# A transformer block pair on one core: late projection chunks between the first attention pairs, the product with V between a pair's transposes

## The reference

```
h = rms_norm(x);  qa, ka, va, qb, kb, vb = split(h @ w_in)        # 12 chunks of 128 columns
qa, ka = rope(rms_norm per head);  qb, kb = rope                  # 8 + 8 query heads, 2 + 2 kv heads of 64
out_a = softmax(qa ka' / 8) va                                    # all 512 keys
out_b = softmax over |kpos - qpos| <= 128, with a sink logit per head
mixed = concat(rms_norm(out_a), rms_norm(out_b)) @ w_out          # the two group norms
x = x + rms_norm(mixed);  x = x + rms_norm(ffn(rms_norm(x)))
second block: pooling and stick-breaking attention, gated ffn, x = x + sigmoid(rms_norm(x) @ w) * (p @ w_p)
result = rms_norm(x)
```

## Time and profile before

| | us |
|---|---|
| median of three runs | 1353.02 |
| the profiled execution | 1354.36 |
| its span in the trace | 1350.8 |
| TensorE matmul busy | 1317.9 (98%) |
| VectorE busy | 663.6 (49%) |
| ScalarE busy | 540.3 (40%) |
| GpSimd busy | 114.2 (8%) |

### The profile page before, as it was taken

One profiled execution on the slowest core, in us unless ns is written; L12 is line 12 of the kernel. 1 busy time (PEld: TensorE's weight loads), 2 busy tenths in 40 slices (PEclk: granted clock), 3 DMA queues, 4 the chain that ended last, 5 costly groups with the idle time before them and its releaser, 6 DMA issues.

```text
span 1350.8 us, 14769 instructions
## 1 busy us (share of the span) xinstructions
PE 1317.9 (98%) x6132; PEld 1054.4 (78%) x6132; DVE 663.6 (49%) x905; ACT 540.3 (40%) x733; POOL 114.2 (8%) x112
## 2 busy tenths in 40 slices
PE   6988989999999999999999999999999999999997
PEld 5863458888888888887888888888888888888876
DVE  6768754663535441226535445563544444423246
ACT  6547864542323232225225555542432232322235
POOL 3000113400000001003000001011000000000112
PEclk9999999999999999999999999999999999999999
DMA  6110012032232323231322111222232222232321
GB/s 246 63 63 1 1 60 98 32 125 94 94 97 98 107 65 107 86 127 39 132 94 67 62 64 61 91 96 102 96 108 99 94 94 94 69 102 93 110 94 63
DMA packets 20593, 117.73 MB, mean 87 GB/s; under 512 B 2480, under 2 KB 2864, under 8 KB 9904
## 3 DMA queue, kind: packets, MB, share of 16 engines
q1 hardware_dynamic: 19104, 113.75, 24.6%
q10 hardware_dynamic: 1424, 3.06, 0.6%
HBM read 114.70 MB, written 2.10 MB: 86 GB/s over the span
## 4 chain that ended last, share of the span: by engine, by line
PE 94%; DVE 3%; ACT 1%; DMA 1%; issue 0%; POOL 0%; SPq 0%; ACTq 0%; POOLq 0%
PE ps L477 91%; PE ps L684 2%; DMA w_raw<-weights 1%; DVE prob L1364 1%; DVE nmax L1560 1%; DVE w_lo L1360 1%; POOL sqsum L453 0%; ACT w_hi L921 0%; ACT OUT L921 0%; DVE hf L1367 0%; DVE hf L1360 0%; ACT hf L921 0%; PE ps L560 0%; PE ps L552 0%; ACT sq L921 0%
## 5 line engine op out<-in xcount | busy, mean ns | idle before, releaser
L477 PE MATMUL ps<-h_hi,w_hi 128*128 128x512 f32 (+1 forms) x1256 | 493.3, 393 | 13.1 <-DVE w_lo L1360 12.0
L477 PE MATMUL ps<-h_lo,w_hi 128*128 128x512 f32 (+1 forms) x1256 | 488.6, 389 | 0.0
L477 PE MATMUL ps<-h_hi,w_lo 128*128 128x512 f32 (+1 forms) x1256 | 488.5, 389 | 0.0
L1360 DVE TENSOR_TENSOR w_lo<-w_raw,w_hi 128x2048 fp32r<-128x2048 f32 (+2 forms) x117 | 242.1, 2072 | 274.0 <-ACT w_hi L921 274.0
L477 PEld LDWEIGHTS ps<-h_hi,w_hi 128*128 128x128 f32 x1256 | 236.6, 188 | 66.8 <-issue 13.2
L921 ACT ACTIVATE w_hi<-w_raw 128x2048 fp32r<-128x2048 f32 (+2 forms) x117 | 201.2, 1722 | 199.6 <-DMA w_raw<-weights 199.4
L477 PEld LDWEIGHTS ps<-h_hi,w_lo 128*128 128x128 f32 x1256 | 236.5, 188 | 49.3
L477 PEld LDWEIGHTS ps<-h_lo,w_hi 128*128 128x128 f32 x1256 | 236.6, 188 | 48.7 <-issue 1.0
L453 POOL TENSOR_TENSOR sqsum<-sqsum,sq 128x512 f32<-128x512 f32 x66 | 95.8, 1451 | 987.4 <-ACT sq L921 985.6
L477 PE MATMUL ps<-mid_hi,w_hi 128*128 128x512 f32 x352 | 136.9, 389 | 0.0
L477 PE MATMUL ps<-mid_lo,w_hi 128*128 128x512 f32 x352 | 136.9, 389 | 0.0
(11 more groups left out here) (183 smaller groups left out, 1083.4 us busy)
## 6 DMA issues: line engine op xcount, KB each, us to landing
w_raw<-weights SPq DMA_DIRECT2D x81, 1024.0 KB, 4.9
w_raw<-weights SPq DMA_DIRECT2D x32, 704.0 KB, 4.1
X<-x_t SPq DMA_DIRECT2D x3, 512.0 KB, 8.3
c<-constants ACTq DMA_DIRECT2D x1, 1280.0 KB, 8.8
w_raw<-weights SPq DMA_DIRECT2D x4, 256.0 KB, 8.3
wp_raw<-weights SPq DMA_DIRECT2D x1, 1024.0 KB, 6.9
out<-OUT SPq DMA_DIRECT2D x4, 256.0 KB, 2.7
out<-OUT ACTq DMA_DIRECT2D x4, 256.0 KB, 2.7
```

The costliest lines, as they stand in the source:

```text
L477: return nc.tensor.matmul(out, lhsT, rhs, start=start, stop=stop, skip_group_check=loose)
L1360: return nc.vector.tensor_tensor(out, a, b, op)
```

## The change

The last three projection chunks leave the line and stand between the first pairs: chunk 9 whole in step 0, chunks 10 and 11 in halves of four input tiles in steps 2, 4, 6 and 8, in banks 7, 6, 7. The first two score pairs come right after chunk 8. Rope of chunk 8 also becomes pieces in the loop. The splits of the first two output projection units move: on ScalarE to steps 1 and 4, on VectorE to the end of the loop. From step 11 on, `weighted` runs at odd steps, that is between the two transposes of a pair. The sums of squares of the two group norms no longer go through GpSimd: TensorE adds each tile with eight one-column matmuls (`sum_part`), for group a in steps 45 to 48, for group b two in steps 60 and 62 and two after the loop; the third and fourth square wait for the sums before the previous one. The last product with V waits for the last transposed rows, and not for a copied output. At the end SP issues all eight stores in the order (0,0), (1,0), (0,1), ...; the last half's square moves to VectorE; GpSimd adds one tile less and TensorE one more; VectorE's second half of factors comes before its second output.

```diff
-NORM_A_STEP = 44
+NORM_A_STEP = 43
+SQUARES_B = (60, 62)
+LATE_BANKS = (7, 6, 7)
+LATE_PARTS = {0: (9, 0, 8), 2: (10, 0, 4), 4: (10, 4, 8), 6: (11, 0, 4), 8: (11, 4, 8)}
-LATE_ROPE, LATE_TR, LATE_V = {9: 4, 10: 13}, 23, 25
+LATE_ROPE, LATE_TR, LATE_V = {8: (2, 3, 3, 4), 9: (4, 5, 6, 6), 10: (7, 8, 8, 9)}, 23, 25
...
@@ SP
-            for n, (b, part) in enumerate(((1, 0), (1, 1), (3, 0), (3, 1))):
+            for n, (b, part) in enumerate(((0, 0), (0, 1), (2, 0), (2, 1))):
+                sp.wait_ge(out_act, n + 1)
+                sp.dma_start(*store(b, part)).then_inc(out_stored, 16)
                 sp.wait_ge(out_ready, n + 1)
-                sp.dma_start(*store(b, part)).then_inc(out_stored, 16)
+                sp.dma_start(*store(b + 1, part)).then_inc(out_stored, 16)
@@ TensorE
+            def sum_part(nm, j):
+                pe.wait_ge(*nm.squares(j + 1))
+                for b in range(NB):
+                    last = mm(ps[:, nm.ss_bank, b:b + 1], sq[:, j % 2, b * P:(b + 1) * P], ones[:, 0:1],
+                              j == 0 and b == 0, True, loose=True)
+                last.then_inc((nm.total if j == nm.n - 1 else nm.summed).sem, 1)
...
-            for u in range(1, UNITS_IN1):
-                unit("in1", u, 2 * u, 2, KS, h_hi, h_lo, after=beside, hooks={11: {4: lambda: scores(0)}})
+            for u in range(1, UNITS_IN1 - 1):
+                unit("in1", u, 2 * u, 2 if u < 4 else 1, KS, h_hi, h_lo, after=beside)
+            scores(0)
+            scores(1)
+            def late_part(j, k0, k1):
+                u = j // 2
+                if k0 == 0:
+                    if j == 9:
+                        pe.wait_ge(*n_mix_pre.factor_used)
+                    elif j == 10:
+                        pe.wait_ge(lo_ready, u)
+                        pe.wait_ge(roped, ROPED.index(NORMED[-1]) + 1)
+                    else:
+                        pe.wait_ge(evac_act, EVAC["in1", 9][1])
+                for k in range(k0, k1):
+                    last = three(BANK["in1", j], u % SLOTS, j % 2 * KD + k, h_hi[:, k, :], h_lo[:, k, :],
+                                 k == 0, k == KD - 1)
+                if k1 == KD:
+                    last.then_inc(group_done, 1)
...
-                if s >= 10 and s % 2 == 0:
-                    weighted((s - 10) // 8, (s - 10) % 8 // 2)
+                if s in LATE_PARTS:
+                    late_part(*LATE_PARTS[s])
+                if s == 0:
+                    spread_heads(len(NORMED) - 1)
+                if s >= 10 and s % 2:
+                    weighted((s - 11) // 8, (s - 11) % 8 // 2)
...
-                if s == NORM_A_STEP + 4:
-                    total(n_group_a)
+                if 2 <= s - NORM_A_STEP < 6:
+                    sum_part(n_group_a, s - NORM_A_STEP - 2)
+                if s in SQUARES_B:
+                    sum_part(n_group_b, SQUARES_B.index(s))
...
-                pe.wait_ge(ot_ready, 8)
-                total(n_group_b)
+                sum_part(n_group_b, 2)
+                sum_part(n_group_b, 3)
...
+            pe.wait_ge(*n_final.squares(KD - 1))
+            final_part(0, sq[:, 0, :])
+            final_part(1, sq[:, 0, :])
@@ ScalarE
             def square(nm, j, src):
                 if j >= 2:
-                    act.wait_ge(*nm.summed(j))
+                    act.wait_ge(*nm.summed(j - 1 if nm.kind == "split" else j))
...
+                if s == 4:
+                    split(UNITS_IN1 + 1)
                 if s == 1:
+                    split(UNITS_IN1)
+                    evacuate(9)
+                if s == 5:
+                    evacuate(10)
+                if s == 9:
                     evacuate(11)
...
+                if s + 2 in SQUARES_B:
+                    square_group(n_group_b, 4, SQUARES_B.index(s + 2))
...
-                act.wait_ge(out_act, b + part + 1)
-                act.dma_start(*store(b, part)).then_inc(out_stored, 16)
-            half_square(1)
@@ VectorE
-            split(UNITS_IN1 + 1)
+                if s == 1:
+                    finish_normed(LATE1 - 2)
...
+            split(UNITS_IN1)
+            split(UNITS_IN1 + 1)
             variance(n_group_b, 4 * P)
...
+            dve.wait_ge(half_added, 2)
+            dve.wait_ge(*n_final.squares(KD))
+            tt(sq[:, 1, half_of(1)], X[:, KD - 1, half_of(1)], X[:, KD - 1, half_of(1)], ALU.mult
+               ).then_inc(n_final.squares.sem, 1)
             half_variance(0)
             half_scale(1)
             half_factors(0)
             half_variance(1)
             dve.wait_ge(*n_final.root(1))
             turned_out(1, 0)
+            half_factors(1)
             turned_out(1, 1)
-            half_factors(1)
```

More of the change, by code:

```diff
@@ L294, in __init__ @@
                  self.hi, self.lo) = (Count(norm_sems[e], norm_counts[e]) for e in NORM_EVENTS)
-                self.sums = n + (kind == "wide")
+                self.kind = kind
+                self.sums = n - 1 if kind == "split" else n - (kind == "final") + (kind == "wide")
                 n_f32 = {"split": n, "late": 1, "wide": 1, "added": n, "final": 0}[kind]
@@ L329, in build @@
                 bank = j + 2 if phase in ("ff1", "in2") and 4 <= j < 6 else j % banks
+                if phase == "in1" and j >= LATE1:
+                    bank = LATE_BANKS[j - LATE1]
                 if phase == "in2" and j >= 14:
@@ L364, in vee_bank, with spread_bank @@
             return 4 if j < LATE1 else SIDE_BANK
+        def spread_bank(n):
+            return 4 if n < len(NORMED) - 1 else HSUM_BANK
         def tr_bank(s):
@@ L445, in sum_squares @@
             def sum_squares(nm):
+                if nm.kind == "split":
+                    return
                 if nm.before is not None:
@@ L858, in _ @@
                      hooks={2: {3: lambda: wide_total(n_ple)}})
+            sqsum_all = sqsum[:, :]
             def final_part(i, src):
@@ L862, in final_part @@
                     last = mm(ps[:, SUM_BANKS[i], b:b + 1], src[:, b * P:(b + 1) * P], ones[:, 0:1],
-                              src is sums and b == 2 * i, True, loose=True)
+                              src is sqsum_all and b == 2 * i, True, loose=True)
                 return last
@@ L886, in _ @@
                         turn(b, 0)
-            sums, square = sqsum[:, :], sq[:, 1, :]
-            pe.wait_ge(*n_final.summed(KD))
-            final_part(0, sums)
-            final_part(1, sums)
+            square = sq[:, 1, :]
+            pe.wait_ge(*n_final.summed(KD - 1))
+            final_part(0, sqsum_all)
+            final_part(1, sqsum_all)
+            pe.wait_ge(*n_final.squares(KD - 1))
+            final_part(0, sq[:, 0, :])
+            final_part(1, sq[:, 0, :])
             pe.wait_ge(*n_final.squares(KD))
@@ L1043, in evacuate @@
                 af(y_of(j), ps[:, BANK["in1", j], :], ACT.Copy).then_inc(evac_act, 1)
-            for j in range(11):
-                if j in (3, 5, 7, 9):
+            for j in range(LATE1):
+                if j in (3, 5, 7):
                     split(j // 2 + 2)
@@ L1544, in _ @@
             late_marks = {}
-            for j in range(1, LATE1):
+            for j in range(1, LATE1 - 1):
                 rope(j)
```

65 lines of the change are left out of this document (35 added, 30 removed).

## The result

The changed kernel took 1357.58 us (median of 5 runs, 1357.49 to 1359.28); the kernel before, beside it, 1352.88 us (5 runs, 1352.28 to 1354.19). The ratio is 1.0036, 95% interval 1.0026 to 1.0047: slower by about 4.7 us, where 1353.7 was forecast. The profiled execution took 1359.28 us (span 1357.2), 1.7 above the median.

A forecast was written before the change was run, and what follows sets the result against it. TensorE was taken to bound the kernel, so only its idle time and its work could matter. Terms -8.7 + 2.2 + 2.7 + 3.2 + 0.5 + 0.8 = +0.7 gave 1353.7 us, range 1349.5 to 1357.5.

The forecast's parts named there:

- Part 1: Three projection chunks moved into the first attention pairs fill TensorE's hole at the front: -8.7 us.
- The second rival: ScalarE late in the early pairs behind a late weight landing for split 7: +2.1, 1355.8 or more; chance 0.18.
- Part 2: Product with V between the transposes: +2.2 us in steps 10 to 31, +2.7 in windowed steps 32 to 63.
- the windowed steps: Steps 32 to 63 outside the group sums: pairs bound by TensorE and pairs after copies lose time, +2.7 us.
- The 0.17 ahead of a product after transposes: In each full pair, a load after transposes starts 0.17 us late; the pair takes 3.28 us instead of 3.10.
- waits behind a copied output: Every eighth step, ScalarE's output copy delays the exponential and stalls TensorE: 0.53 us, and 0.78 at step 25.
- Part 3: Group sums on TensorE: +3.2 us for group a, with ScalarE's squares waiting for sums, and +0.5 for group b.
- the second wait of a square: Group a: ScalarE's fourth square waits for TensorE's sum one step after the third: another 1.0 us.
- Group b: Two of its sums on TensorE at steps 60 and 62, partly offset by shorter waits: +0.5 us.
- Part 4: The end: with DMA engines full, the first store is issued later, from one queue: +0.8 us.
- The alternative put beside it: By issue time alone, the end would come 0.8 us earlier and the whole sum 1.6 lower.
- Third, the clock: Rival: clock falls to half in a stretch like 176.9 to 185.2, adding 5.3 us of TensorE work: 1359; chance 0.04.

The follow-up runs named there:

- the kernel with both edits: Changed kernel with group a's squares 2 and 3 in buffers of their own and four 256-column matmuls in each of steps 46 and 47: 1353.48 us.
- the two fills: Changed kernel plus, in each of steps 46 and 47, four 256-column matmuls (1354.47 us) or nine one-column matmuls (1363.31 us).
- own buffers: Changed kernel with group a's third and fourth square in buffers of their own, so ScalarE does not wait for TensorE's sums: 1353.24 us.
- GpSimd's sum: Changed kernel with group a's four squares summed by GpSimd again and one TensorE reduction after step 48: 1349.19 us.
- the old order, product first: Changed kernel with the product with V ahead of both transposes again, at even steps from 10 on: 1349.18 us.
- only the chunks: Only three projection chunks moved between the first pairs; product ahead of both transposes, both groups summed by GpSimd, end as before: 1346.01 us.

## Why the prediction was wrong

**Part 1** was right: -9.1 for -8.7. TensorE works without a hole from 72 to 100. The second rival, a late landing, did not happen.

**Part 2** was right. Steps 10 to 31 cost +2.0 for +2.2, and the windowed steps 1.7 (32 to 43) and 0.8 (50 to 54 at full clock, 6.34 for 5.51), 2.5 for 2.7. The 0.17 ahead of a product after transposes is nearly all there: 3.24 for the 3.28 worked out. The first two waits behind a copied output were 0.44 and 0.70, for 0.53 and 0.78.

**Part 3** was right where the clock was full. The transposes of step 46 came at 5.38 for 5.4. Group b: 1138.95 for 1138.36, +0.6 for +0.5. The loads, with whatever the new order costs there, come to 1.1 for 1.7 in the kernel with both edits; the second wait of a square has no price at full clock, and I leave the term at 3.2.

**Part 4** was right: +0.75 for +0.8. The alternative put beside it, an end 0.8 earlier by issue time, did not come: seven ends as in the changed kernel are 0.75 later than six as before. The Trainium skill (Trainium Kernel Development and Optimization, Key Constraints) says only that several issuers save issue time, and the traces agree with it: from the first store to the end passed 6.9 us with one queue as with two, in all profiles but one. No run changed the number of queues by itself.

**What failed is the rival "Third, the clock", and with it the sum, which takes every term at clock 1.00.** It had 0.04, placed in the stretch that VectorE owns, with the argument that the old rows show 1.00 through transposes, one-column sums and 3 us of idle time. They did, each by itself. The prediction looked for no other place, though the change put two extra waits, sixteen more one-column loads and small transposes next to each other; there the clock fell for 17 us. Its price: steps 44 to 50 took 17.29 for 12.6, steps 50 to 54 took 7.93 for the 6.34 at full clock: 4.7 + 1.6 = 6.3, and 1.6 more in the profiled execution's end. With the measured terms, -9.1 + 2.0 + 2.5 + 3.2 + 0.6 + 0.75, the change at full clock is worth 0.0; with the clock +6.3. The runs show +4.7. Of the difference, 0.5 to 1 is time around the span (below); the rest is likely the start, which two profiles can't settle. The forecast of 1353.7 is what the terms give at full clock to within 0.7, so the sum failed by the clock alone.

That the clock is the cause and not a by-product is shown by the two fills: more work and full clock, 1354.5; as much more work in one-column matmuls, 1363.3. That the fall needs the wait of the squares is refuted by the kernel with own buffers. GpSimd's sum, own buffers and the old order, each by itself, made the fall shorter or rarer, and none kept its profile at 1.00, so what share the waits, the one-column loads and the order have is not shown. What stays open is why one kernel falls in some executions and not in others (own buffers, product first, only the chunks), and why the kernel before, whose steps 54 to 58 take the same 7.95, was at 1.00 in both of its profiles.

## What to carry to other kernels

A row of tiny matmuls on TensorE can cost more than its own time, and by the runs here a stall likely can too, because the matmuls behind it may run at half clock: price an edit that thins TensorE's work twice, once at each clock, and give the second a real chance even where each ingredient is seen at full clock in the old trace. Work moved onto the critical engine to spare an idle one (here GpSimd's adds) needs its reason measured; here putting it back was worth 8.4 us. Where a wait can't be removed, a few wide matmuls into unused columns in it were free where they fitted, and likely paid for themselves; where they did not fit (four in each of steps 46 and 47) they cost 1.5 and gave back more.

## What the runs showed that was not expected

**Half clock outlasts what went ahead of it.** In the changed kernel TensorE was idle for 0.97 us ahead of the fall and for 0.41 in it, busy 15.59 of 16 us, and the clock came back only at 178. The kernel with one-column fills was busy 20.00 of 20.00 us at 0.50.

**An early fall, and where the start lies.** Eleven of the fourteen profiles, both of the kernel before among them, have one more stretch of 3.4 us at half clock ahead of the pairs, which the rows of the attention stage don't show. In the kernel before it ran from 34.2 to 37.6 with TensorE busy all the time, in its second profile from 21.2 to 24.6. In the five profiles with it at 33 or 34 us P lies at 73.2 to 73.9, in the other nine at 70.7 to 72.1. So most of the 2 us by which the start moves goes with where this fall lies; no run set it on purpose.

**Something outside the span.** Device time less span was 1.7 to 2.1 us in each run of eleven kernels, but 2.0 to 4.7 in those of the kernel before (medians 2.43, 2.88 and 2.74 in the three groups) and 2.5 to 3.5 in those with only the chunks moved. In the windows of the kernel before the DMA engines move something more after the span's end at 1350.8 (last columns: share, GB/s); the changed kernel has the like ahead of its stores:

```profile
1352.00:1353.00 1.00, 0.00 (x0) 0.00 (x0) 0.00 (x0) 0.00 (x0) 0.00 (x0) 0.50 0.00 0
1353.00:1354.00 1.00, 0.00 (x0) 0.00 (x0) 0.00 (x0) 0.00 (x0) 0.00 (x0) 0.50 0.12 25
```

```profile
1341.00:1342.00 1.00, 1.00 (x11) 1.00 (x9) 0.42 (x1) 0.51 (x2) 0.07 (x1) 1.00 0.06 16
```

Between 1340 and the end each of the two instruction queues has one packet in both (16 and 8 KB), so this is likely a load of code. Its 16 KB packet comes at 1353.1 in this profile of the kernel before, after the last store, and in the changed one at 1341.6, 9 us before the first. In the kernel with only the chunks moved it comes after the end too, at 1345.3 for an end at 1342.9. The difference is worth 0.5 to 1 us in favour of the changed kernel and was in no term. No run moved it by itself.

**The stores.** From first store to the end of the span passed 6.9 us in every profile but the second of the kernel before (8.8), with one issuing queue as with two; the engines moved about 400 GB/s in the full microseconds. In that one the last 2.5 us move only 20 to 27 GB/s, and the 16 KB instruction packet comes at 1343.5, 1.6 us behind its first store; that it is the cause was not tried.
